# Moving the decay gate's small products and the query norms inside a hand-written schedule

## The reference, cut to what matters

```python
g_f = jax.nn.log_sigmoid((lr_f @ wa2_f + ba_f)) / 16      # lr: 256 x 16, wa2: 16 x 512
g_b = jax.nn.log_sigmoid((lr_b @ wa2_b + ba_b)) / 16
b = jnp.cumsum(g, axis=3)                                 # within chunks of 64 tokens
a = einsum(q * exp(b - b_ref), k * exp(b_ref - b))        # and q * exp(b), k * exp(b_last - b)
qa = rope(rms_norm(q_a.reshape(B, T, 8, 128), q_norm_g), pos)   # attention's queries, a norm per head
```

## Time and profile before

| | |
|---|---|
| median of 3 runs | 2164.28 us (2164.04 to 2165.69) |
| profiled execution | 2165.07 us, span 2163.4 us from first to last instruction |
| TensorE matmul busy | 2145.8 us (99%) |
| VectorE busy | 1444.6 us (67%) |
| ScalarE busy | 1115.7 us (52%) |
| GpSimd busy | 48.3 us (2%) |
| DMA, mean over the span | 182 GB/s |
| mean granted TensorE clock | 0.999 |

### The profile page before, as it was taken

The page is one execution under the profiler, slowest core; times in us unless marked ns, Lnnn a source line. Parts: engine busy times, 40 slices in busy tenths (PEclk is TensorE's granted clock), DMA queues, the critical chain, the costliest instruction groups (busy, mean ns, idle before and its releaser), DMA issues.

```text
span 2163.4 us, 28495 instructions
## 1 busy us (share of the span) xinstructions
PE 2145.8 (99%) x9902; PEld 1786.5 (83%) x9902; DVE 1444.6 (67%) x2009; ACT 1115.7 (52%) x1459; POOL 48.3 (2%) x59
## 2 busy tenths in 40 slices
PE   9999999999999999999999999999999999999999
PEld 7897888888888888888888877888888888888887
DVE  5899977676667666444656457567868787784443
ACT  6556665444444444444456436555665666653433
POOL 1000000000000000000000042000000000000000
PEclk9999999999999999999999999999999999999999
DMA  7665355666666666665555544466665666556564
GB/s 226 192 181 169 126 186 153 201 191 195 193 193 191 195 190 210 198 193 193 162 170 150 175 121 140 146 185 185 185 201 169 201 185 198 182 189 203 192 191 167
DMA packets 216389, 393.18 MB, mean 182 GB/s; under 512 B 13711, under 2 KB 58329, under 8 KB 216059
## 3 DMA queue, kind: packets, MB, share of 16 engines
q1 hardware_dynamic: 216139, 391.13, 59.3%
q10 hardware_dynamic: 176, 1.06, 0.2%
HBM read 390.04 MB, written 2.10 MB: 181 GB/s over the span
## 4 chain that ended last, share of the span: by engine, by line
PE 94%; DVE 3%; ACT 1%; issue 1%; POOL 0%; ACTq 0%; DVEq 0%; POOLq 0%
PE ps L544 30%; PE ps L546 29%; PE ps L545 29%; DVE w_lo L1783 1%; PE ps L582 1%; DVE cv L1895 0%; PE ps L1133 0%; PE ps L961 0%; PE ps L980 0%; PE ps L606 0%; DVE fac L2256 0%; ACT w_hi L1171 0%; PE ps L708 0%; PE ps L562 0%; PE ps L564 0%
## 5 line engine op out<-in xcount | busy, mean ns | idle before, releaser
L1783 DVE TENSOR_TENSOR w_lo<-raw,w_hi 128x1024 fp32r<-128x1024 f32 (+2 forms) x761 | 898.9, 1189 | 605.5 <-ACT w_hi L1171 597.6
L1171 ACT ACTIVATE w_hi<-raw 128x1024 fp32r<-128x1024 f32 (+2 forms) x761 | 778.3, 1030 | 755.5 <-PE ps L546 717.9
L544 PE MATMUL ps<-w_hi,hT_hi 128*128 128x512 f32 (+2 forms) x2192 | 856.5, 391 | 3.8 <-DVE w_lo L1783 3.2
L546 PE MATMUL ps<-w_hi,hT_lo 128*128 128x512 f32 (+2 forms) x2192 | 847.0, 386 | 0.0
L545 PE MATMUL ps<-w_lo,hT_hi 128*128 128x512 f32 (+2 forms) x2192 | 846.4, 386 | 0.0
L544 PEld LDWEIGHTS ps<-w_hi,hT_hi 128*128 128x128 f32 x2192 | 412.1, 188 | 87.1 <-issue 6.3
L546 PEld LDWEIGHTS ps<-w_hi,hT_lo 128*128 128x128 f32 x2192 | 411.9, 188 | 79.0
L545 PEld LDWEIGHTS ps<-w_lo,hT_hi 128*128 128x128 f32 x2192 | 412.3, 188 | 75.4
L544 PE MATMUL ps<-w_hi,aT_hi 128*128 128x512 f32 x688 | 267.7, 389 | 0.0
L546 PE MATMUL ps<-w_hi,aT_lo 128*128 128x512 f32 x688 | 267.7, 389 | 0.0
L545 PE MATMUL ps<-w_lo,aT_hi 128*128 128x512 f32 x688 | 267.6, 389 | 0.0
(11 more groups left out here) (293 smaller groups left out, 1102.3 us busy)
## 6 DMA issues: line engine op xcount, KB each, us to landing
raw<-in_w_up SPq DMA_DIRECT2D x264, 512.0 KB, 3.8
raw<-in_w_down SPq DMA_DIRECT2D x160, 512.0 KB, 4.6
raw<-in_w_gate SPq DMA_DIRECT2D x88, 512.0 KB, 4.4
raw<-in_w_in SPq DMA_DIRECT2D x80, 464.0 KB, 3.5
raw<-in_w_out SPq DMA_DIRECT2D x64, 512.0 KB, 4.0
raw<-in_w_in SPq DMA_DIRECT2D x64, 256.0 KB, 3.4
raw<-in_w_in SPq DMA_DIRECT2D x24, 448.0 KB, 3.7
raw<-in_w_down SPq DMA_DIRECT2D x32, 256.0 KB, 3.0
```

Source lines behind the costliest of these rows:

```text
L544: pe.matmul(o, xh, wh, start=first, stop=False)
L546: mm = pe.matmul(o, xl, wh, start=False, stop=last)
L1171: act.activation(w_hi[:, s, :kc, :width], raw[:, s, :kc, :width], ACT.Copy).then_inc(hi_ready, 1)
L1783: dve.tensor_tensor(w_lo[:, s, :kc, :width], raw[:, s, :kc, :width], w_hi[:, s, :kc, :width].bitcast(F32), ALU.subtract).then_inc(lo_ready, 1)
```

## The change

TensorE issues the four low-rank products one before each of tiles 16, 17, 18 and 19, where they stood together before tile 16. ScalarE's and VectorE's positions around the gate move by one or two tiles. VectorE issues one split after each of the eight factor multiplications, where two of them in each four had one. In OUT2 the squares of `qb` and `qc` move on ScalarE from slot 3, ahead of the first exponential, to slot 4, behind it; the means move from slot 4 to 5, the norms from slots 5 and 6 to 6 and 7, and the first `half_add` from slot 6 to 7.

```diff
@@ TensorE, IN2
                 for t in range(TOK):
                     mm = pe.matmul(ps[:, 4 + 2 * d + t, :], lrT[:, d, t * P:(t + 1) * P], wa2[:, d, :],
                                    start=True, stop=True)
-            mm.then_inc(gl_mm, 1)
-            in2_tiles(16, 28)
+                    if (d, t) == (1, TOK - 1):
+                        mm.then_inc(gl_mm, 1)
+                    in2_tiles(16 + 2 * d + t, 17 + 2 * d + t)
+            in2_tiles(20, 28)
@@ ScalarE, IN2
             z2_block(1)
-            hi_upto(T_IN2 + 20)
+            hi_upto(T_IN2 + 22)
 
             act.wait_ge(gl_dve, 1)
             for d in range(2):
                 ins = act.activation(gb[:, 0, d], gb[:, 0, d], ACT.Exp)
                 if d == 0:
-                    hi_upto(T_IN2 + 21)
+                    hi_upto(T_IN2 + 23)
             ins.then_inc(gl_act, 1)
-            hi_upto(T_IN2 + 22)
+            hi_upto(T_IN2 + 24)
             act.wait_ge(gl_act, 2)
             for d in range(2):
                 ins = act.activation(gb[:, 0, d], gb[:, 0, d], ACT.Ln, bias=1.0)
                 if d == 0:
-                    hi_upto(T_IN2 + 23)
+                    hi_upto(T_IN2 + 25)
             ins.then_inc(gl_act, 1)
             hi_upto(T_IN2 + 27)
@@ ScalarE, OUT2
-                if g == 3:
+                if g == 4:
                     part_squares(2)
                     part_squares(3)
@@ VectorE, IN2
-            lo_upto(T_IN2 + 19)
+            lo_upto(T_IN2 + 21)
             dve.wait_ge(gl_mm, 2)
...
             step(ins)
-            lo_upto(T_IN2 + 20)
+            lo_upto(T_IN2 + 22)
...
             ins.then_inc(gl_dve, 1)
-            lo_upto(T_IN2 + 23)
+            lo_upto(T_IN2 + 24)
             dve.wait_ge(gl_act, 3)
...
                     ins = dve.tensor_tensor(fac[:, d, i], fac[:, d, i], src[:], ALU.mult)
-                    if i % 2 == 0:
-                        lo_upto(done[0] + 1)
+                    lo_upto(done[0] + 1)
@@ VectorE, OUT2
-                if g == 4:
+                if g == 5:
                     dve.wait_ge(sq_done, 10)
                     mean_sq("qb", HD)
                     mean_sq("qc", HD)
-                if g in (5, 6):
-                    part_norm(g - 3)
+                if g in (6, 7):
+                    part_norm(g - 4)
...
-                if g % 4 == 2 and 1 <= g // 4 <= 4:
+                if g in (7, 10, 14, 18):
                     half_add(T_OUT2 + 4 * (g // 4), g // 4 - 1, half_added)
```

## The result

The changed kernel takes 2169.43 us (median of 19 runs, 2167.46 to 2172.64), the kernel before 2165.24 us (19 runs, 2164.00 to 2167.62). The ratio is 1.0018, 95% interval 1.0012 to 1.0024: slower by some 0.18%, 4.2 us, just inside the 0.2% that I called no change, though the interval reaches beyond it, and outside the range of 2162.5 to 2167.6. The profiled execution after took 2167.80 us (span 2166.1), against 2165.07 (span 2163.4): 2.7 us more.

The account below looks back on a forecast made before the run. TensorE, with a matmul under way for 99% of the span, was taken as the bound. Interruptions +0.8, clock -1.6, chain +5.2, factors -2.1 and OUT2 -2.2 summed to +0.1 us; forecast 2165.0 us, range 2162.5 to 2167.6.

Parts of the forecast that it names:

- The chain through VectorE and ScalarE: Gate behind the low-rank products: less tile cover makes TensorE wait 1.8 and 3.3 us ahead of tiles 22 and 24, +5.2 us.
- The clock: Behind the low-rank products: spread between full tiles, they no longer let the granted clock fall to 1.2 GHz, -1.6 us.
- Rival B: Gate: the clock falls in the new wait, another slow stretch of 1.6 us, 2166.6 us in all; chance 0.18.
- OUT2: Attention stage: both waits for exponentials go, split_rest is late next with a 1.6 us wait; -2.2 us, bounds -4.2 and 0.
- Interruptions: Low-rank products: three more interruptions of TensorE's stream at 0.26 us each, +0.8 us, bounds 0 and 1.2.
- Factors: Factor stage, tiles 39 to 41: one split per factor removes TensorE's lost time, -2.1 us, bounds -2.1 and 0.
- A: Gate: the wait isn't there, three spread tiles still cover the chain; +5.2 goes, 2160.0 us; chance 0.12.
- C: Gate: each 17-row product alone lets the clock fall; four slow stretches give 2171.4 us, three 2169.8; chance 0.06.
- D: Factor stage: the factor edit does nothing because loads bind, 2167.1 us; chance 0.08.

## Why the prediction was wrong

**The chain through VectorE and ScalarE: right.** Cover counted in tiles gave waits of 1.8 and 3.3 us ahead of tiles 22 and 24, 5.2 with restarts. The trace has 1.8 and 3.4, at these tiles, and moving one split or the products' place earlier changes them as the count says (2.7 for 2.7; no wait). The block moved late has the second wait and, through its slow stretch, 0.3 of the first.

**The clock: the step that failed.** "I expect the clock to hold: -1.6 us." Behind the products it held, in each trace that has them spread. But the sum took the 1.6 us as won, and put the clock behind the new waits at nothing. Rival B, the fall in the new wait, to which I gave 0.18, is what the profile shows: 0.57 at 1141 to 1145. So the term was 0 in the two profiled executions. The forecast for the profiled execution, 2165.2, plus this 1.6 and the two sizes below, +1.0 and +0.4, is 2168.2; less the 0.4 of tiles 28 to 35 it is the 2167.8 that was measured.

Two things about the clock I hadn't seen. The fall before was not in each execution: 11 of 72 runs had 1.000, and one trace with the block has no fall behind it. And OUT2's remaining wait, forecast at 1.6 us and measured at 2.8, can let the clock fall too. No run of the changed kernel, of 29, had 1.000. In the medians the term therefore has the other sign: of their 4.2 us the account explains 3.1, and the other 1.1 fits a clock that falls more often in the changed kernel. The forecast had -1.6 there.

The Trainium skill, "TensorE: Matmul & The Clock Gate", Why this matters for your kernels, warns of idle gaps between bursts; I had cited it against the change and priced what it warns of as a rival. The traces bear the warning out behind 3.2 us of idle time, in three of four, and they show falls behind shorter gaps than the one that the page names: behind 2.8 us in two of four, and behind layer 1's 1.9 us in seven of 14. Here the measurement decides: no wait of 1.9 us or more was safe, and none was sure to let the clock fall. Nor need TensorE be idle: a block of 17-row products that kept it "busy" for 3.5 us let the clock fall in seven of the eight traces that have such a block.

**OUT2: mechanism right, size wrong.** The two waits for exponentials went, `split_rest` was late next. The term was -2.2 and measured -1.2: meetings with GpSimd cost VectorE 3.4 us ahead of `split_rest`, and the durations of before that my walk used had 2.4 of them (norms 1.4, splits 0.5, a sum 0.5). Leaving out the turn brings each of these steps back to its shorter duration and removes the wait, which shows the cause.

**Interruptions:** +0.8 forecast, +1.2 measured: 0.39 us each instead of 0.26. **Factors:** -2.1, as forecast, and alone as well.

**Rivals A, C and D** did not occur: the waits are there, single 17-row products between full tiles leave the clock at 1.00, and the factor edit works. The chance of 0.79 for a move under 0.2% fits the 0.18% measured, but only just. The range was too narrow since I didn't let B and OUT2's bound come together, and had only three runs to go by, which spread by 1.7 us, where 19 spread by 3.6.

## What to carry to other kernels

When work is spread between the steps of a stream to protect one thing, count the cover behind its last piece, in steps of the stream, against the chain that it releases: each step by which the last piece moves later takes one step off the cover of everything behind it. Spread to earlier places, so that the last piece stays where it stood. Price what the clock may do behind each wait that the change adds, beside what it gives back. After a wait has been moved, look at what is queued ahead of the next one on the same engine, with its duration beside the other engines' work, not alone.

## What the runs showed of the hardware

- The granted clock fell to 1.2 GHz behind 3.5 us of 17-row products with TensorE busy throughout, and behind idle times of 3.2, 2.8 and 1.9 us, each in some executions and not in others. In the gate and in OUT2 most falls cost 1.6 us; one that began during the wait cost 2.7. The 1.9 us are layer 1's, behind small products of 128 columns. Behind the gate's waits of 1.5 and OUT2's of 1.8 us no trace here shows a fall.
- Executions of the same kernel fall into groups by mean granted clock, 0.7 to 2.9 us apart. Comparing runs of equal clock helps to size an edit where less than 0.2% matters, but with one or two runs to a group it was off by about 1 us either way (2.9 and 4.9 for one kernel), and the rounded mean doesn't tell two slow stretches from three. TensorE's starts in the stage of the edit say more than either.
- VectorE's norms (two inputs in SBUF) took 1.14 us for four alone and 2.73 beside GpSimd's turn, 1.14 again in the same place with the turn left out. A 128 x 2 `tensor_scalar` took 0.63 beside it instead of 0.17.
